# One 512-column matmul in place of two 256-column ones for the high weights of four stages

## The chip, the cores and the metric

The kernel runs on one NeuronCore of a Trainium2 chip. The metric is the device time in microseconds of one execution; smaller is better.

## What is computed

A four-layer model on one sequence of 256 tokens, 2048 channels wide, in float32. Layers 0 and 1 are gated mixers with an inner width of 4096, layers 2 and 3 are hybrid layers with three branches. The lines of the reference that touch the change:

```python
for i in range(2):                                   # layers 0 and 1
    h = rmsnorm(x, g_pre[i])
    u, z = split(h @ w_in[i])                        # each 256 x 4096
    if i == 0:
        y = pool_mixer(u, ...)    # trailing means - u, then 4 groups: d @ w_grp (1024x1024), (y + b) * scale
    else:
        y = rglru(causal_depthwise_conv(u, ...), ...)
    y = y * silu(z)
    o = y @ w_out[i]                                 # 4096 -> 2048
    x = x + rmsnorm(o, g_post[i])
    gate = sigmoid(rmsnorm(x, g_ple_in[i]) @ w_ple_gate[i])
    x = x + rmsnorm((p[i] @ w_ple[i]) * gate, g_ple_out[i])
# layers 2 and 3
    merged = sum over 3 branches of sigmoid(gate_b) * (y_b @ w_branch[b])
    x = x + merged @ w_out
```

## The kernel before

**Products.** Every matrix product has float32 accuracy from three products of numbers with fewer bits. A weight is split into a high part `w_hi` and a low part `w_lo` (what is left), an activation likewise: its tile holds the high part of 256 tokens in columns 0 to 255 and the low part in columns 256 to 511. The sum is w_hi x high + w_hi x low + w_lo x high. A tile is 128 input channels by 128 output channels. For each tile of weights the function `products` issues L589 (w_hi past the high part), L590 (w_hi past the low part) and L600 (w_lo past the high part), 256 columns each, and all three add into the same 256 columns (half) of one PSUM bank.

**Units.** The weights stream from HBM in 1144 units of 8 tiles (128 x 1024 values, 512 KB) through four slots. SyncE loads a unit into `raw`, ScalarE writes `w_hi` (`split_hi`, L1056) once PE has left the slot, and VectorE writes `w_lo` (`split_lo`, L1522) after it. Both run three units ahead of PE. Within a unit PE does all eight tiles' high matmuls first and then the eight low ones, if the tiles belong to one product.

**Stages.** A stage is a list of products, done in a number of turns. `depth` is the number of tiles that one product sums.

| stage | layers | turns x products x depth | units | who reads the product before |
|---|---|---|---|---|
| window, conv | 0, 1 | 8 x 4 x 16 | 64 | VectorE |
| pooled | 0 | 4 x 8 x 8 | 32 | VectorE, one operation: (product + b) * scale into `wide` |
| silu | 0 | 8 x 4 x 16 | 64 | VectorE times `rstd_x` into `val`, ScalarE tanh |
| lru | 1 | 4 x 24 products of two depths | 80 | both |
| squared (w_out) | 0, 1 | 4 x 4 x 32 | 64 | ScalarE: times g_post into `o_buf`, square into `val`; POOL sums |
| plain, gate | 0, 1 | | 36 | both |
| stages by token and by feature | 2, 3 | | 288 a layer | both |
| wo | 2, 3 | 4 x 4 x 16 | 32 | VectorE: `x_buf` += 0.5 * product |

In the first turn of wo, and of layer 1's squared, `first_turn` goes by input channel over the four products (L730, L732, L752 in place of L589, L590, L600); their order within a unit is the same.

**Stages by token.** gv, vb, uv, mix_gate and mix_branch have activations as the stationary operand and weights as the moving one. They use matmuls of 512 columns (L648 with `w_hi`, L665 with `w_lo`): 8 and 4 for a unit. `four_runs` reads the moving operand in runs of four columns, 32 runs for each of four weight tiles; the output is a whole bank in order. `pace` (L631) and `settle` (L610) put in one matmul of 208 or two of 128 columns whose result nobody reads.

**Order of the other engines.** In each unit ScalarE first does `split_hi` for the unit three ahead, and then what it reads for products that end in this unit (`events`). VectorE does `split_lo`, then `first` (it reads the product, L1958 in pooled, L1965 in silu, L1999 in wo), and then `second`, the rest of an earlier tile. In squared ScalarE reads twice (L1388, L1390) and POOL adds to `acc` (L2372). PE waits for a bank's last reader before it starts a product there (`occupant`). Pooled and silu rotate over four banks, squared over seven (`banks` and `pm`); wo has a list, WO_BANKS.

## Time and profile before

| | us |
|---|---|
| median of the runs | 3237.09 |
| lowest, highest of 3 | 3233.3, 3238.89 |
| span of the profiled execution | 3231.5 |
| PE (matmul) busy | 3224.2 |
| VectorE busy | 2245.0 |
| ScalarE busy | 1673.9 |
| GpSimd busy | 745.3 |

The profile is of one execution. The span runs from its first to its last instruction and holds no launch. Matmuls are pipelined: a row's duration reaches into the next matmul, so the spacing between starts tells what one costs. `x8` at the end of a row says that eight matmuls of one line were merged.

### The profile page before, as it was taken

What the parts mean: (1) busy time and instruction counts of PE and PEld (TensorE: products, weight loads), DVE (VectorE), ACT (ScalarE), POOL (GpSimd) and SP (SyncE); (2) the same over time, 40 slices, a digit from 0 to 9 for tenths busy, and PEclk for the clock granted to TensorE, in tenths of its full rate; (3) what the DMA queues carried; (4) which work ended last, traced back from release to release, by engine and by line L of the source; (5) the groups of instructions that cost most, each with busy time, mean ns of one, the idle gap of its engine ahead of it and who ended that gap; (6) DMA issues with size and microseconds to landing.
All of it is one profiled execution on the core that took longest, in us unless ns stands there. A gap on an engine that the chain in (4) does not pass through costs nothing.

```text
span 3231.5 us, 57755 instructions
## 1 busy us (share of the span) xinstructions
PE 3224.2 (100%) x24078; PEld 3067.1 (95%) x24078; DVE 2245.0 (69%) x2890; ACT 1673.9 (52%) x2082; POOL 745.3 (23%) x784
## 2 busy tenths in 40 slices
PE   9999999999999999999999999999999999999999
PEld 9999999999999999999899988889999999888889
DVE  7986654588888844887978655555568887555554
ACT  5344444565588844655655444444456554444443
POOL 2632320054544400332423200000114332000000
PEclk9999999999999999999999999999999999999999
DMA  7565665556666565555555566665665554666665
GB/s 248 183 203 191 195 225 195 178 190 216 196 194 192 196 224 194 188 191 195 169 182 170 170 196 199 193 201 193 194 201 174 177 176 157 195 196 198 194 198 174
DMA packets 171316, 621.66 MB, mean 192 GB/s; under 512 B 19376, under 2 KB 21424, under 8 KB 170672
## 3 DMA queue, kind: packets, MB, share of 16 engines
q1 hardware_dynamic: 165888, 601.96, 57.4%
q10 hardware_dynamic: 4880, 14.97, 1.2%
q8 instruction: 190, 3.11, 0.4%
q0 software_dynamic: 288, 1.05, 0.1%
q14 instruction: 70, 0.57, 0.1%
HBM read 611.61 MB, written 5.24 MB: 191 GB/s over the span
## 4 chain that ended last, share of the span: by engine, by line
PE 99%; DVE 1%; DMA 0%; ACT 0%; issue 0%; ACTq 0%; DVEq 0%
PE banks L648 20%; PE banks L600 13%; PE banks L589 13%; PE banks L590 13%; PE banks L665 10%; PE pm L600 5%; PE pm L589 5%; PE pm L590 5%; PE banks L752 2%; PE banks L730 2%; PE banks L732 2%; PE pm L752 2%; PE pm L732 2%; PE pm L730 2%; PE pm L800 0%; PE pm L926 0%
## 5 line engine op out<-in xcount | busy, mean ns | idle before, releaser
L1522 DVE TENSOR_TENSOR w_lo<-raw,w_hi 128x1024 fp32r<-128x1024 f32 x1144 | 1469.9, 1290 | 857.9 <-ACT w_hi L1056 851.5
L1056 ACT ACTIVATE w_hi<-raw 128x1024 fp32r<-128x1024 f32 x1143 | 1204.3, 1058 | 1089.7 <-PE banks L665 460.9
L589 PE MATMUL banks<-xs,w_hi 128*128 128x256 f32 x2468 | 579.4, 277 | 0.0
L590 PE MATMUL banks<-xs,w_hi 128*128 128x256 f32 x2468 | 578.1, 277 | 0.0
L648 PE MATMUL banks<-w_hi,xs 128*128 128x512 f32 x2048 | 493.5, 381 | 0.0
L590 PEld LDWEIGHTS banks<-xs,w_hi 128*128 128x128 f32 x2468 | 463.8, 188 | 0.3
L589 PEld LDWEIGHTS banks<-xs,w_hi 128*128 128x128 f32 x2468 | 463.8, 188 | 0.3
L648 PEld LDWEIGHTS banks<-w_hi,xs 128*128 128x128 f32 x2048 | 383.8, 188 | 68.2
L600 PE MATMUL banks<-xs,w_lo 128*128 128x256 f32 x2468 | 338.8, 279 | 0.0
L600 PEld LDWEIGHTS banks<-xs,w_lo 128*128 128x128 f32 x2468 | 305.7, 188 | 3.6 <-issue 2.5
L665 PE MATMUL banks<-w_lo,xs 128*128 128x512 f32 x1024 | 270.6, 384 | 0.0
L589 PE MATMUL pm<-xs,w_hi 128*128 128x256 f32 x956 | 223.3, 276 | 0.0
L590 PE MATMUL pm<-xs,w_hi 128*128 128x256 f32 x956 | 223.3, 276 | 0.0
L665 PEld LDWEIGHTS banks<-w_lo,xs 128*128 128x128 f32 x1024 | 190.2, 188 | 32.6
L590 PE MATMUL banks<-inner,w_hi 128*128 128x256 f32 x896 | 211.0, 276 | 0.0
L589 PE MATMUL banks<-inner,w_hi 128*128 128x256 f32 x896 | 211.0, 276 | 0.0
L648 PE MATMUL banks<-w_hi,y_abc 128*128 128x512 f32 x768 | 184.3, 380 | 0.0
L589 PEld LDWEIGHTS pm<-xs,w_hi 128*128 128x128 f32 x956 | 179.5, 188 | 0.0
L590 PEld LDWEIGHTS pm<-xs,w_hi 128*128 128x128 f32 x956 | 179.5, 188 | 0.0
L589 PEld LDWEIGHTS banks<-inner,w_hi 128*128 128x128 f32 x896 | 168.2, 188 | 0.0
L590 PEld LDWEIGHTS banks<-inner,w_hi 128*128 128x128 f32 x896 | 168.2, 188 | 0.0
L648 PEld LDWEIGHTS banks<-w_hi,y_abc 128*128 128x128 f32 x768 | 144.1, 188 | 24.8
(405 smaller groups left out, 5418.1 us busy)
## 6 DMA issues: line engine op xcount, KB each, us to landing
raw<-weights SPq DMA_DIRECT2D x1143, 512.0 KB, 3.6
wide<-x_in ACTq DMA_DIRECT2D x1, 2048.0 KB, 8.8
x_scratch<-wide ACTq DMA_DIRECT2D x1, 2048.0 KB, 12.5
wide<-x_scratch ACTq DMA_DIRECT2D x1, 2048.0 KB, 9.3
wide<-x_in ACTq DMA_DIRECT2D x3, 512.0 KB, 6.6
out_x<-wide SPq DMA_DIRECT2D x3, 512.0 KB, 5.4
g_v<-x_scratch ACTq DMA_DIRECT2D x2, 512.0 KB, 4.9
w_st<-w_s ACTq DMA_DIRECT2D x2, 512.0 KB, 4.6
```

Of the source, the lines that this page charges most:

```text
L589: nc.tensor.matmul(bank, w_hi[:, slot, w], x[:, 0:T], start=(k + t == 0), stop=False)
L590: nc.tensor.matmul(bank, w_hi[:, slot, w], x[:, T:2 * T], start=False, stop=False)
L600: ins = nc.tensor.matmul(bank, w_lo[:, slot, w], p.operand(i, k + t)[:, 0:T], start=False, stop=(k + t == p.depth - 1))
L648: nc.tensor.matmul(product_bank(s, i, j), x[:, at:at + P], four_runs(w_hi[:, slot, w]), start=(k == 0 and at < T), stop=False)
L665: ins = nc.tensor.matmul(product_bank(s, i, j), x[:, j * P:(j + 1) * P], four_runs(w_lo[:, slot, w]), start=False, stop=(k == depth - 1))
L730: nc.tensor.matmul(bank, w_hi[:, slot, w], operand[:, k, 0:T], start=(k == 0 and j < 4), stop=False, skip_group_check=True)
L732: nc.tensor.matmul(bank, w_hi[:, slot, w], operand[:, k, T:2 * T], start=False, stop=False, skip_group_check=True)
L752: ins = nc.tensor.matmul(bank, w_lo[:, slot, w], operand[:, k, 0:T], start=False, stop=(k == s.products[0].depth - 1), skip_group_check=True)
L1056: nc.scalar.activation(w_hi[:, slot, :], raw[:, slot, :], ACT.Copy).then_inc(hi_done, 1)
L1522: nc.vector.tensor_tensor(w_lo[:, slot, :], raw[:, slot, :], w_hi[:, slot, :].bitcast(F32), ALU.subtract).then_inc(lo_done, 1)
```

## The change

In four stages the two matmuls with the same high weights become one of 512 columns, that streams the whole activation tile (high and low part) past them. Its output is a whole bank: the high part's product in the first half, to which the low weights' product is still added, and the low part's in the second half. Whoever reads the product adds the halves. It holds for all of pooled and silu, for the first three of four turns of squared, and for all products of wo but the last; the others stay as they were. In silu, squared and wo both the moving operand and the output are addressed in runs of four columns (`in_runs`: 4 x 32 runs of 4 from each half of 256, with the same order on both sides, so that each value lands where it would without it); in pooled both are addressed in order.

The reading of a product:
- pooled: ScalarE reads the low half into `low_part` with scale and the bias `pool_shift` (= pool_b * pool_scale, made once by VectorE), VectorE waits for that (`low_read`) and does high half * scale + `low_part`.
- silu: ScalarE copies the low half, VectorE adds the high half and multiplies by `rstd_x` in a second operation, ScalarE's tanh follows in the next unit (`finish_wide`).
- squared: ScalarE copies the low half, VectorE adds into `whole`, ScalarE makes `o_buf` and the square in the next unit, POOL's sum waits for the square (`squares_made`).
- wo: VectorE updates `x_buf` twice, once with each half.

```diff
+    def wide(self, i, j):
+        if self.name == "squared":
+            return i < 3
+        if self.name == "wo":
+            return (i, j) != (3, 3)
+        return self.name in ("pooled", "silu")
...
+def in_runs(a, name):
+    return a if name == "pooled" else a.rearrange("p (g c f) -> p c g f", c=4, f=4)
...
-            stage("squared", ..., ND // 4, "p", readers="AAAA")
+            stage("squared", ..., ND // 4, "p", readers="DDDD" * 3 + "AAAA")
...
+        def whole_bank(s, i, j):
+            b = s.bank(i, j)
+            return banks[:, b, :] if b < BANKS else pm[:, b - BANKS, :]
...  (products, and likewise first_turn)
+                            if s.wide(i, j):
+                                nc.tensor.matmul(in_runs(whole_bank(s, i, j), s.name), w_hi[:, slot, w], in_runs(x, s.name),
+                                                 start=(k + t == 0), stop=False, skip_group_check=True)
+                                continue
                             nc.tensor.matmul(bank, w_hi[:, slot, w], x[:, 0:T], start=(k + t == 0), stop=False)
                             nc.tensor.matmul(bank, w_hi[:, slot, w], x[:, T:2 * T], start=False, stop=False)
...  (ScalarE)
+                        while low_parts_read:
+                            finish_wide(*low_parts_read.pop(0))
...
+                            if s.name != "wo" and s.wide(i_, j):
+                                read_low_part(i_, j)
+                                if s.name != "pooled":
+                                    low_parts_read.append((i_, j))
+                                continue
...
+                def read_low_part(i, j):
+                    m = i * s.width + j
+                    sc.wait_ge(pe_mark, product_end(s, i, j))
+                    slot = len(low_parts) % 2
+                    if len(low_parts) >= 2:
+                        sc.wait_ge(*read_of(*low_parts[-2]))
+                    low_parts.append((s, i, j))
+                    part = whole_bank(s, i, j)[:, T:2 * T]
+                    if s.name == "pooled":
+                        sc.wait_ge(shift_made, 1)
+                        ins = nc.scalar.activation(low_part[:, slot, :], part, ACT.Identity,
+                                                   scale=col("pool_scale", m), bias=pool_shift[:, m:m + 1])
+                    else:
+                        ins = nc.scalar.activation(low_part[:, slot, :], part, ACT.Copy)
+                    ins.then_inc(low_read, 1)
+
+                def finish_wide(i, j):
+                    m = i * s.width + j
+                    sc.wait_ge(*read_of(s, i, j))
+                    wait(sc, pool_done, m + (s.base["p"] - 3))
+                    if s.name == "silu":
+                        nc.scalar.activation(act[:, j % 4, :], val[:, j % 4, :], ACT.Tanh, scale=0.5)\
+                            .then_inc(act_ready, 1)
+                    else:
+                        nc.scalar.activation(o_buf[:, m, :], whole[:, j, :], ACT.Copy, scale=col(f"g_post{l}", m))
+                        nc.scalar.activation(val[:, j, :], whole[:, j, :], ACT.Square).then_inc(squares_made, 1)
...  (VectorE)
                     elif s.name == "pooled":
-                        nc.vector.tensor_scalar(wide[:, m, :], product(s, i, j), col("pool_b", m),
-                                                col("pool_scale", m), ALU.add, ALU.mult)\
+                        ve.wait_ge(low_read, low_base + m + 1)
+                        nc.vector.scalar_tensor_tensor(
+                            out=wide[:, m, :], in0=product(s, i, j), scalar=col("pool_scale", m),
+                            in1=low_part[:, (low_base + m) % 2, :], op0=ALU.mult, op1=ALU.add).then_inc(dve_read, 1)
+                    elif s.name == "silu":
+                        ve.wait_ge(low_read, low_base + m + 1)
+                        link(nc.vector.tensor_tensor(v, product(s, i, j), low_part[:, (low_base + m) % 2, :], ALU.add))
+                        nc.vector.tensor_tensor(v, v, rstd_x[:], ALU.mult).then_inc(dve_read, 1)
...
                     elif s.name == "wo":
-                        nc.vector.scalar_tensor_tensor(
-                            out=x_buf[:, m, :], in0=product(s, i, j), scalar=0.5, in1=x_buf[:, m, :],
-                            op0=ALU.mult, op1=ALU.add).then_inc(dve_read, 1)
+                        parts = [product(s, i, j)]
+                        if s.wide(i, j):
+                            parts.append(whole_bank(s, i, j)[:, T:2 * T])
+                        for part in parts:
+                            ins = nc.vector.scalar_tensor_tensor(
+                                out=x_buf[:, m, :], in0=part, scalar=0.5, in1=x_buf[:, m, :], op0=ALU.mult, op1=ALU.add)
+                            if part is not parts[-1]:
+                                link(ins)
+                        ins.then_inc(dve_read, 1)
```

## Rows read from the trace of the kernel before

**Rows 1.** The page: busy us (share of the span) xinstructions of each engine.
```profile
PE 3224.2 (100%) x24078; PEld 3067.1 (95%) x24078; DVE 2245.0 (69%) x2890; ACT 1673.9 (52%) x2082; POOL 745.3 (23%) x784
```

**Rows 2.** The page: the chain that ended last, share of the span by engine.
```profile
PE 99%; DVE 1%; DMA 0%; ACT 0%; issue 0%; ACTq 0%; DVEq 0%
```

**Rows 3.** Busy time by stretch (us, each engine (x), PEclk, DMA, GB/s): pooled, silu, squared, wo.
```profile
181.70:269.00 87.30, 87.30 (x773) 87.30 (x772) 64.06 (x93) 34.24 (x34) 6.37 (x7) 1.00 0.62 200
269.00:443.30 174.30, 174.30 (x1540) 174.30 (x1539) 115.67 (x158) 77.54 (x95) 63.28 (x61) 1.00 0.60 193
443.30:617.60 174.30, 174.30 (x1540) 174.30 (x1539) 80.79 (x69) 78.32 (x96) 14.42 (x20) 1.00 0.62 208
...
2223.20:2311.20 88.00, 88.00 (x778) 87.99 (x777) 54.57 (x65) 41.43 (x48) 2.44 (x1) 1.00 0.60 192
```

**Rows 4.** Timeline of PE in silu (start us, us, what): low matmuls of successive units.
```profile
300.96 1.07 PE L600 MATMUL banks<-xs,w_lo 128*128 128x256 f32 x8
303.68 1.07 PE L600 MATMUL banks<-xs,w_lo 128*128 128x256 f32 x8
```

**Rows 5.** Timeline of PE in mix: the pace matmul and two units after it.
```profile
1846.55 0.26 PE L631 MATMUL pm<-xs,w_hi 128*128 128x208 f32 x1
...
1847.54 1.92 PE L648 MATMUL banks<-w_hi,xs 128*128 128x512 f32 x8
...
1850.18 1.92 PE L648 MATMUL banks<-w_hi,xs 128*128 128x512 f32 x8
```

**Rows 6.** Timeline of PE where za (256 columns) gives way to mix (512).
```profile
1839.42 1.94 PE L648 MATMUL banks<-w_hi,xs 128*128 128x512 f32 x8
1841.20 1.05 PE L665 MATMUL banks<-w_lo,xs 128*128 128x512 f32 x4
1842.10 1.95 PE L648 MATMUL banks<-w_hi,xs 128*128 128x512 f32 x8
```

**Rows 7.** Timeline of PE where uv (512, settled) gives way to zc (256).
```profile
1629.50 1.05 PE L665 MATMUL banks<-w_lo,latent 128*128 128x512 f32 x4
...
1632.22 1.07 PE L600 MATMUL banks<-xs,w_lo 128*128 128x256 f32 x8
```

**Rows 8.** Timeline of PE where gv (512, unsettled) gives way to latent (256).
```profile
2405.31 1.05 PE L665 MATMUL banks<-w_lo,xs 128*128 128x512 f32 x4
...
2408.02 1.07 PE L600 MATMUL banks<-xs,w_lo 128*128 128x256 f32 x8
```

**Rows 9.** Groups by line and shape: silu, then 1742 to 1752 us in za.
```profile
L589 PE MATMUL banks<-xs,w_hi 128*128 128x256 f32 x512 | 119.2, 276 | 0.0
...
L589 PE MATMUL banks<-xs,w_hi 128*128 128x256 f32 x24 | 5.8, 281 | 0.0
```

**Rows 10.** Groups by line and shape, readers: one each of pooled, squared, wo.
```profile
L1958 DVE TENSOR_SCALAR wide<-banks,chan 128x256 f32<-128x256 f32 x31 | 16.8, 543 | 8.4 <-PE banks L600 8.3
...
L1388 ACT ACTIVATE wide<-banks,chan 128x256 f32<-128x256 f32 x9 | 4.3, 475 | 14.1 <-PE banks L600 14.1
...
L1999 DVE SCALAR_TENSOR_TENSOR wide<-banks,wide 128x256 f32<-128x256 f32 x9 | 3.7, 422 | 2.4 <-PE banks L600 2.0 <-PE pm L752 0.3
```

**Rows 11.** Groups by line and shape in silu: both splits and the reader.
```profile
L1522 DVE TENSOR_TENSOR w_lo<-raw,w_hi 128x1024 fp32r<-128x1024 f32 x64 | 78.6, 1227 | 46.9 <-ACT w_hi L1056 46.9
...
L1056 ACT ACTIVATE w_hi<-raw 128x1024 fp32r<-128x1024 f32 x64 | 67.5, 1055 | 33.0 <-PE banks L600 33.0
...
L1965 DVE TENSOR_TENSOR val<-banks,rstd_x 128x256 f32<-128x256 f32 x31 | 13.2, 426 | 10.4 <-PE banks L600 10.4
```

**Rows 12.** Timelines of ScalarE, VectorE and PE in pooled: one unit's splits and use.
```profile
195.57 1.06 ACT L1056 ACTIVATE w_hi<-raw 128x1024 fp32r<-128x1024 f32 x1 [1.66 <-PE banks L600]
...
196.66 1.23 DVE L1522 TENSOR_TENSOR w_lo<-raw,w_hi 128x1024 fp32r<-128x1024 f32 x1 [0.61 <-ACT w_hi L1056]
...
203.47 0.28 PE L589 MATMUL banks<-inner,w_hi 128*128 128x256 f32 x1
...
205.28 1.07 PE L600 MATMUL banks<-inner,w_lo 128*128 128x256 f32 x8
```

More of the change, by code:

```diff
@@ L100, in __init__, with readers_to @@
         self.by_token = name in BY_TOKEN
+    def wide(self, i, j):
[4 more added lines that the diff above has]
+        return self.name in ("pooled", "silu")
+    def readers_to(self, e, m):
+        if len(self.readers) > self.width:
+            return self.readers[:m].count(e)
+        turns, j = divmod(m, self.width)
+        return turns * self.readers.count(e) + self.readers[:j].count(e)
     def bank(self, i, j):
@@ L236, in build @@
         y_abc, merged = place("y_abc", 0, [P, 24, 2 * T], F32R), place("merged", 48, [P, ND, 2 * T], F32R)
+        low_part, whole = place("low_part", 104, [P, 2, T]), place("whole", 106, [P, 4, T])
+        pool_shift = place("pool_shift", 110, [P, NI])
         sq_sum = place("sq_sum", 40, [P, 4, T])
@@ L355, in build @@
                       readers="AAAADD" * 4)
-            stage("squared", [Product(NI, from_inner) for _ in range(4)], ND // 4, "p", readers="AAAA")
+            stage("squared", [Product(NI, from_inner) for _ in range(4)], ND // 4, "p", readers="DDDD" * 3 + "AAAA")
             stage("plain", [Product(NP_, lambda turn, k: xs[:, ND - NP_ + k, :]) for _ in range(16)], 1, "",
@@ L394, in build @@
             for e in read0:
-                read0[e] += s.turns * s.readers.count(e)
+                read0[e] += s.readers_to(e, s.turns * s.width)
             for c in s.signals.split():
@@ L454, in read_of @@
         def read_of(s, i, j):
[L456 to L457 removed]
+            m = i * s.width + j
+            e = s.readers[m if len(s.readers) > s.width else j]
+            return READ[e], s.read0[e] + s.readers_to(e, m + 1)
         def read_end(s):
@@ L600, in products @@
                             ins = nc.tensor.matmul(bank, w_lo[:, slot, w], p.operand(i, k + t)[:, 0:T],
-                                                   start=False, stop=(k + t == p.depth - 1))
+                                                   start=False, stop=(k + t == p.depth - 1),
+                                                   skip_group_check=s.wide(i, j))
                         ins.then_inc(pe_mark, 1)
@@ L729, in first_turn @@
                         bank, w = product_bank(s, j // 4, j % 4), slice(c * P, (c + 1) * P)
+                        if s.wide(0, j):
+                            nc.tensor.matmul(in_runs(whole_bank(s, 0, j), s.name), w_hi[:, slot, w], in_runs(operand[:, k, :], s.name),
+                                             start=(k == 0), stop=False, skip_group_check=True)
+                            continue
                         nc.tensor.matmul(bank, w_hi[:, slot, w], operand[:, k, 0:T], start=(k == 0 and j < 4),
@@ L1498, in _ @@
                     turn(i)
+                while low_parts_read:
+                    finish_wide(*low_parts_read.pop(0))
                 if s.name == "conv":
@@ L1957, in first @@
                     elif s.name == "pooled":
-                        nc.vector.tensor_scalar(wide[:, m, :], product(s, i, j), col("pool_b", m),
-                                                col("pool_scale", m), ALU.add, ALU.mult)\
+                        ve.wait_ge(low_read, low_base + m + 1)
[6 more added lines that the diff above has]
+                        nc.vector.tensor_tensor(v, v, rstd_x[:], ALU.mult).then_inc(dve_read, 1)
+                    elif s.name == "squared":
+                        if not s.wide(i, j):
+                            return
+                        ve.wait_ge(low_read, low_base + m + 1)
+                        if i:
+                            ve.wait_ge(squares_made, l * 12 + m - 3)
+                        nc.vector.tensor_tensor(whole[:, j, :], product(s, i, j), low_part[:, (low_base + m) % 2, :], ALU.add)\
                             .then_inc(dve_read, 1)
-                    elif s.name in ("silu", "gate", "za", "zc", "zb", "ub", "latent"):
+                    elif s.name in ("gate", "za", "zc", "zb", "ub", "latent"):
                         if s.name in ("latent", "ub"):
@@ L2235, in _ @@
                 window_rest, half_done = half_done, []
+                if s.name == "pooled":
+                    nc.vector.tensor_tensor(pool_shift, col("pool_b", 0, NI), col("pool_scale", 0, NI), ALU.mult)\
+                        .then_inc(shift_made, 1)
                 for i in range(s.turns):
                     turn(i)
+                if s.name in ("pooled", "silu", "squared"):
+                    low_base += sum(s.wide(*divmod(m, s.width)) for m in range(s.turns * s.width))
                 while half_done and s.name != "window":
@@ L2370, in post @@
                     elif s.name == "squared":
-                        gp.wait_ge(*read_of(s, i, j))
+                        if s.wide(i, j):
+                            gp.wait_ge(squares_made, l * 12 + m + 1)
+                        else:
+                            gp.wait_ge(*read_of(s, i, j))
                         nc.gpsimd.tensor_tensor(acc[:], acc[:], val[:, j, :], ALU.add).then_inc(pool_done, 1)
```

8 lines of the change are left out of this document (5 added, 3 removed).

## The prediction

> **What bounds the kernel now.** I read the page's busy line first: TensorE is busy for 3224.2 of 3231.5 us, VectorE 69%, ScalarE 52% [rows 1]. The chain that ended last agrees: 99% of it is PE [rows 2]. So the question is what one matmul costs, and whether the change makes PE wait for anybody. The table by stretch for one stage of each changed kind (the second squared and wo look the same) shows PE busy without a hole, at the full granted clock, while VectorE is idle for 23 of 87 us in pooled, 59 of 174 in silu, 94 of 174 in squared, 33 of 88 in wo, and ScalarE for more [rows 3]. So what counts is PE's spacing, from one start to the next; its "mean ns" overlaps the next matmul.
>
> Then the timeline of PE. A narrow unit (8 tiles, each two high matmuls and one low one of 256 columns) takes 303.68 - 300.96 = 2.72 us [rows 4], so 2720 / 24 = 113.3 ns per matmul. The stages by token show the 512-column form, with the moving operand already in runs of four: 12 matmuls in 1850.18 - 1847.54 = 2.64 us, 220 ns each [rows 5]. Streaming is 256/2.4 = 106.7 and 512/2.4 = 213.3 ns, so each matmul pays 6.7 ns on top, whatever its length. This is all that the change can win: 2 x 113.3 - 220 = 6.7 ns for each pair replaced.
>
> **How many.** A turn of pooled, silu, squared and wo has 8, 16, 16 and 8 units. Pooled changes in 4 turns, 32 units; silu in 4 turns of 4 products (32 tiles of 16 depth), 64; squared in 3 of 4 turns in each of two layers, 96; wo in all but the last product, 30 in each of two layers, 60. Sum 252 units of 8 pairs, 2016 pairs. At the full price: 8 x 6.7 = 53 ns a unit, 252 x 53 = 13.4 us.
>
> **What takes part of it away: the crossings.** Now all matmuls of these stages have one length. Afterwards each unit is 8 wide, then 8 narrow: it crosses from one length to the other twice. The trace has such crossings at the edges of the stages by token.
> - Narrow to wide: the first 8 wide ones after a narrow stretch take 1841.20 - 1839.42 = 1.78 us instead of 1.76, and the unit 2.68 instead of 2.64 [rows 6]: 223 ns each. The wide stream has a settled spacing (220) and an unsettled one (223), and after a narrow stretch it begins in the second. Price: 20 ns for 8.
> - Wide to narrow, from the settled spacing: from the fourth-last wide start to the 17th narrow one 1632.22 - 1629.50 = 2.72 us, where 4 x 220 + 16 x 113.3 = 2.693 [rows 7]: 27 ns.
> - Wide to narrow, from the unsettled spacing: 2408.02 - 2405.31 = 2.71 us, where 4 x 223 + 16 x 113.3 = 2.705 [rows 8]: 5 ns.
>
> In a changed unit the wide run of 8 follows a narrow run, so it is unsettled when it ends; the third row is nearer to it than the second. So a changed unit costs 8 x 220 + 8 x 113.3 + 20 + 5 = 2692 ns against 2720: **28 ns saved**, and 252 x 28 = **7.1 us**. With the second crossing at 27 ns it is 2714, 6 ns saved, 1.5 us in all. These are the ends for this term.
>
> The narrow stream has two spacings too: the groups show a mean of 276 ns where it is settled, and 281 in a stretch of za, after attention's matmuls; the difference is its spacing, some 118 against 113 [rows 9]. If the 8 low matmuls of a unit stayed there, the unit would be 8 x 223 + 8 x 118 = 2728, 8 ns more than now, 252 x 8 = +2.0 us. The rows of the crossings speak against it: there the narrow run after a wide one is back at 113 within a few matmuls.
>
> TensorE: Matmul & The Clock Gate, section Back-to-back issue gap, in the Trainium skill, gives a fixed part of about 2.5 ns for an isolated matmul, not 6.7. By that a pair saves 2.5 ns, the change 2016 x 2.5 = 5.0 us, and the time would be near 3232. The same section has a sustained spacing of some 131 ns at 512 columns; no row here is near it, the trace has 220.
>
> **What VectorE and ScalarE get to do.** All of it lies beside PE.
> - Pooled, per unit: ScalarE reads the low half with scale and bias, nearest row 0.475 us [rows 10]; VectorE's 0.543 us operation becomes one with two tensor inputs, like wo's 0.42 [rows 10]. The added wait is VectorE's, for ScalarE's read; queued behind it is the next w_lo split.
> - Silu, per two units: one copy on ScalarE (0.475 again) and one VectorE addition more (0.43, L1965's form [rows 11]); its tanh moves to the next unit.
> - Squared, per four units: a copy and an addition; o_buf and the square are made one unit later, and POOL's sum waits for them. The last turn stays narrow, so the chain after the stage starts from the same last product.
> - Wo: a second 0.42 us update per product, chained, on VectorE. The last product is narrow, so the end of the kernel is as it was.
> - pool_shift is one operation of 32 columns.
>
> Who waits for this is PE, for w_hi and w_lo. Today ScalarE's splits wait for PE, and VectorE's for ScalarE's [rows 11]. In pooled w_hi is split at 195.57 to 196.63 and w_lo at 196.66 to 197.89; PE begins the high part of that unit at 203.47 and the low part at 205.28 [rows 12]. That is 6.8 and 7.4 us ahead. ScalarE's read adds 0.5 us before a split; VectorE's wait adds that and up to one split of 1.06 us. If this cover were gone, each unit would cost what it is late. I take nothing. Per unit of pooled, the fullest case, ScalarE has 1.06 + 0.48 and VectorE 1.25 + 0.42 + a wait of about 1, of 2.69 us. No DMA is moved or added; the stages by token take a unit each 2.64 us with the same loads, so a unit each 2.69 can be fed. A bank is full 512 columns wide now, and as before it is read before its next product. So both ends of this term are 0, unless the first turn of pooled (three left-over window tiles on VectorE) catches PE once or twice: some us at most, inside the range.
>
> **Sum.** On the profiled execution: 3231.5 - 7.1 = 3224.4 us of span. Around the span lie 3237.1 - 3231.5 = 5.6 us to the median of the runs, which stay: **3230.0 us**, 0.22% less. What a measurement of this kernel can tell from no change is about 0.2%, 6.5 us, so this is just beyond it.
>
> **Rivals.**
> - *The full gain.* The wide matmuls run settled and the crossings are free: 13.4 us, 3223.7. For it: in the stages by token the settled spacing is by far the commonest, and a single matmul of another length (pace) puts a stretch there [rows 5]. The crossings seen are between moving operands of different tensors, and the output there is whole; here both differ. Against it: rows 6 and 7.
> - *Nothing is left.* Crossings at 20 + 27 and some late narrow ones: 1.5 us gained to 2.0 lost, 3235.6 to 3239.1. For it: rows 7 is a clean crossing, and its 27 ns can't be told from what a wide run of only 8 does. Against it: the wide run would have to end settled though it began unsettled.
> - *Slower: the output in runs.* In all but pooled (220 units, 1760 wide matmuls) PE now writes its product to the bank in runs of four values with a jump between. No matmul of this size in the trace writes so; only reading in such runs is shown to be free [rows 5]. If each of the 128 runs costs one more cycle, a matmul gets 128/2.4 = 53 ns longer: 1760 x 53 - 7.1 = +86 us, 3323. It turns the result to slower from about (7.1 + 6.5) us / 1760 = 8 ns per matmul, one cycle for every seventh run. PSUM — Partial Sum Buffer, section Specifications (TRN2), in the Trainium skill, speaks for it: any non-contiguous pattern is said to slow matmuls significantly, with lines of 8 bytes. A run of 16 bytes fills two such lines, so the rule may mean single values; no row here decides it.
> - *It doesn't do what it says*: a late split stalls PE. The bound above gives this no place; 0 by the rows.
>
> **Chances.** Part of the gain (the forecast) 0.47, full gain 0.25, nothing left 0.15, slower by the output 0.13. The forecast's own range is 3226 to 3236; its middle is near the 0.2% mark (3230.6), so 0.29 of its 0.47 is faster and 0.18 the same. With the full gain (0.25), faster is 0.54; with the third case, same is 0.33; slower is 0.13, since that case has it all. The range must reach to 3223.7 and to about 3239, and leaves out the slower case and a little more: 3222 to 3239.
>
> **What the profile after would show.** The spacing of L600's eight in pooled, silu, squared and wo: 2.69 us per unit if I am right, 2.667 for the full gain, 2.71 or more for nothing. Between the first wide and the first low matmul of a unit 1.78 us plus the crossing, against 1.76. Wide matmuls of pooled (output whole) and silu (in runs) side by side: if silu's are longer, the output's runs cost. PE without holes in all these stages, else my cover was wrong; and the stages by token unchanged at 2.64 and 2.68. I would be wrong if the crossings within a unit differ from those at the edges of stages.

## The result and the profile after

| | before | after |
|---|---|---|
| median of 15 runs, us | 3235.15 (3233.09 to 3238.89) | 3241.32 (3240.62 to 3243.52) |
| span of the profiled execution, us | 3231.5 | 3239.2 |

The ratio is 1.0021, 95% interval 1.0013 to 1.0028. The change made the kernel 0.2% slower; the forecast was 0.2% faster, and its range ended 2 us too low. The page after, its busy line and the chain's shares by engine; [rows 1, 2] are the same lines of before.

```profile
PE 3232.3 (100%) x22062; PEld 2993.6 (92%) x22062; DVE 2279.9 (70%) x2977; ACT 1708.7 (53%) x2170; POOL 752.8 (23%) x784
...
PE 99%; DVE 1%; ACT 0%; issue 0%; ACTq 0%; DVEq 0%
```

PE has 2016 matmuls fewer (24078 - 22062), as counted in advance, and is busy 8 us longer. The table by stretch for pooled, silu, squared and wo (from:to, us, sum and mean by engine PE, PEld, DVE, ACT, POOL, then granted clock, DMA share, GB/s); [rows 3] is before.

```profile
181.80:270.80 89.00, 89.00 (x516) 77.67 (x515) 62.50 (x94) 48.17 (x65) 6.75 (x7) 1.00 0.60 195
270.80:446.90 176.10, 176.10 (x1029) 155.49 (x1028) 129.72 (x190) 89.82 (x127) 64.49 (x62) 1.00 0.58 192
446.90:622.50 175.60, 175.60 (x1157) 160.14 (x1156) 86.15 (x82) 82.70 (x109) 17.71 (x19) 1.00 0.62 206
...
2229.40:2318.20 88.80, 88.80 (x538) 79.07 (x537) 60.79 (x80) 41.40 (x48) 2.45 (x1) 1.00 0.59 191
```

PE has no hole and the full clock in any of them, as before. Yet the stages are 1.7, 1.8, 1.3 and 0.8 us longer. So nobody makes PE wait: its own matmuls have become dearer than the halves they replace. The timeline of PE shows how: two units of pooled, then two of silu (start us, us, line, what).

```profile
231.08 1.07 PE L633 MATMUL banks<-inner,w_lo 128*128 128x256 f32 x8
232.00 2.02 PE L619 MATMUL banks<-inner,w_hi 128*128 128x512 f32 x8
233.86 1.08 PE L633 MATMUL banks<-inner,w_lo 128*128 128x256 f32 x8
...
330.57 1.09 PE L633 MATMUL banks<-xs,w_lo 128*128 128x256 f32 x8
331.49 1.99 PE L619 MATMUL banks<-xs,w_hi 128*128 128x512 f32 x8
333.32 1.09 PE L633 MATMUL banks<-xs,w_lo 128*128 128x256 f32 x8
334.24 1.99 PE L619 MATMUL banks<-xs,w_hi 128*128 128x512 f32 x8
```

From start to start a unit of pooled takes 233.86 - 231.08 = 2.78 us and one of silu 333.32 - 330.57 = 2.75, against 2.72 before [rows 4]. The eight wide ones take 233.86 - 232.00 = 1.86 us in pooled, 233 ns each, and 333.32 - 331.49 = 1.83 in silu, 229 each. Over all units of a stage the means are 2.773 (pooled) and 2.747 us (silu, the wide turns of squared, wo). So (2.773 - 2.720) x 32 + (2.747 - 2.720) x 220 = 1.7 + 5.9 = **7.6 us**, the 7.7 us of the spans. The narrow stages (2.720) and the stages by token (2.64 and 2.68) are as they were.

The spacing can be read from the groups too, by line and shape; "mean ns" is the spacing plus some 160 (380 stands for 220 in the stages by token). Pooled, silu, and mix of the kernel after:

```profile
L619 PE MATMUL banks<-inner,w_hi 128*128 128x512 f32 x186 | 47.2, 395 | 0.0
...
L619 PE MATMUL banks<-xs,w_hi 128*128 128x512 f32 x439 | 108.9, 388 | 0.0
...
L682 PE MATMUL banks<-w_hi,xs 128*128 128x512 f32 x149 | 35.8, 380 | 0.0
```

The same form, 128x512, has three mean prices: 380 where weights move past activations, 388 where activations move in runs of four, 395 where they move in order.

### The profile page after: what moved, and what is told of

Same layout as the page of the kernel before. It is cut to its first block, busy times and chain, and to the rows that moved or that the text cites. A ratio compares the mean times of both kernels' runs of the same rounds, so it can differ in the third digit from the quotient of the medians.

```text
span 3239.2 us, 54074 instructions
## 1 busy us (share of the span) xinstructions
PE 3232.3 (100%) x22062; PEld 2993.6 (92%) x22062; DVE 2279.9 (70%) x2977; ACT 1708.7 (53%) x2170; POOL 752.8 (23%) x784
## 4 chain that ended last, share of the span: by engine, by line
PE 99%; DVE 1%; ACT 0%; issue 0%; ACTq 0%; DVEq 0%
PE banks L682 20%; PE banks L633 13%; PE banks L699 10%; PE banks L619 10%; PE banks L622 8%; PE banks L623 8%; PE pm L633 5%; PE pm L623 4%; PE pm L622 4%; PE pm L619 3%; PE banks L790 2%; PE pm L790 2%; PE banks L765 1%; PE banks L768 1%; PE pm L770 1%; PE banks L770 1%
## 5 line engine op out<-in xcount | busy, mean ns | idle before, releaser
L622 PE MATMUL banks<-xs,w_hi 128*128 128x256 f32 x1956 | 460.3, 278 | 0.0
L623 PE MATMUL banks<-xs,w_hi 128*128 128x256 f32 x1956 | 459.1, 277 | 0.0
L623 PEld LDWEIGHTS banks<-xs,w_hi 128*128 128x128 f32 x1956 | 368.0, 188 | 0.3
L622 PEld LDWEIGHTS banks<-xs,w_hi 128*128 128x128 f32 x1956 | 367.8, 188 | 0.4
L619 PE MATMUL banks<-inner,w_hi 128*128 128x512 f32 x640 | 160.1, 391 | 0.0
L619 PEld LDWEIGHTS banks<-inner,w_hi 128*128 128x128 f32 x640 | 114.3, 188 | 19.7
L633 PE MATMUL pm<-xs,w_lo 128*128 128x256 f32 x956 | 129.7, 277 | 0.0
L633 PE MATMUL banks<-inner,w_lo 128*128 128x256 f32 x896 | 128.9, 278 | 0.0
```

The lines of the kernel that those rows point to most:

```text
L619: nc.tensor.matmul(in_runs(whole_bank(s, i, j), s.name), w_hi[:, slot, w], in_runs(x, s.name), start=(k + t == 0), stop=False, skip_group_ ...
L622: nc.tensor.matmul(bank, w_hi[:, slot, w], x[:, 0:T], start=(k + t == 0), stop=False)
L623: nc.tensor.matmul(bank, w_hi[:, slot, w], x[:, T:2 * T], start=False, stop=False)
L633: ins = nc.tensor.matmul(bank, w_lo[:, slot, w], p.operand(i, k + t)[:, 0:T], start=False, stop=(k + t == p.depth - 1), skip_group_check=s ...
```

## The experiments

Each edit is made to the kernel after the change, and each run was taken beside one of the kernel before on the same chip. All but e13_held are a single execution, so their units are compared, and no small difference between spans. Unit times are from start to start in PE's timeline. "In runs" is the pattern of `in_runs`, runs of four columns.

### Is it the crossing or the form?

**e1_low_wide_too**, no crossing is left:

```diff
-  matmul(bank, w_lo[:, slot, w], p.operand(i, k + t)[:, 0:T], ...)
+  matmul(in_runs(whole_bank(s, i, j), s.name), w_lo[:, slot, w],
+         in_runs(p.operand(i, k + t), s.name), ...)
```

> The low weights' matmul of the changed stages streams all 512 columns too (it adds low weights times x's low part to the second half, a small term that the reference does not need), so a changed unit is 16 wide matmuls and crosses lengths nowhere. Theory A (crossings: the wide stream is at 220 to 223 ns in long runs, and short runs of eight keep it off that): 3.52 to 3.57 us per unit in pooled, silu, squared and wo alike. Theory B (form: a wide matmul costs 228 ns in runs of four and 233 ns in order because of how it is addressed, whatever stands beside it): 3.65 us in silu, squared and wo, 3.73 us in pooled. Either way the span is longer by some 250 x 0.8 to 0.9 us = 200 to 230 us; that is not the question.

Span 3464.6 us. Timeline of PE, pooled and silu:

```profile
250.10 2.03 PE L619 MATMUL banks<-inner,w_hi 128*128 128x512 f32 x8
251.97 2.03 PE L634 MATMUL banks<-inner,w_lo 128*128 128x512 f32 x8
...
400.50 1.97 PE L619 MATMUL banks<-xs,w_hi 128*128 128x512 f32 x8
402.30 1.98 PE L634 MATMUL banks<-xs,w_lo 128*128 128x512 f32 x8
```

(251.97 - 250.10) / 8 is 233 ns, (402.30 - 400.50) / 8 is 225. Over many units the means are firmer: a unit is 3.733 us in pooled and 3.627 in silu, squared and wo: 16 x 233.3 and 16 x 226.7. With only one length of matmul the high price stays. Theory A (crossings), which had 3.52 to 3.57, falls. The 226.7 is a mean: from start to start the single matmuls of e1's silu take 220, 224, 227, 233 and 229 ns, over and over, and those of its pooled 231 and 236 in turn.

**e2_two_halves** keeps the changed readers and the bank halves, but fills them with two 256-column matmuls:

```diff
-  matmul(in_runs(whole_bank(s, i, j), s.name), w_hi[:, slot, w], in_runs(x, s.name), ...)
+  for half in (slice(0, T), slice(T, 2 * T)):
+      matmul(whole_bank(s, i, j)[:, half], w_hi[:, slot, w], x[:, half], ...)
```

> Everything as in the changed kernel, its readers and waits too, but the wide matmul is split into two of 256 columns, one into each half of the bank. Theories A and B (the time comes from PE's spacing): 2.72 us per unit in the four stages and a span of 3231 to 3233 us, as before the change. Theory C (the readers' extra work on ScalarE and VectorE disturbs PE): units stay at 2.745 us or more and the span at 3239 us.

Its table by stretch for pooled and silu:

```profile
181.70:269.00 87.30, 87.30 (x773) 87.30 (x772) 62.41 (x94) 48.67 (x65) 6.93 (x8) 1.00 0.61 197
269.00:443.30 174.30, 174.30 (x1540) 174.30 (x1539) 129.86 (x190) 89.91 (x127) 63.32 (x62) 1.00 0.60 195
```

PE is busy for the whole of both windows, and as many matmuls fell into them as before (773 and 1540 [rows 3]), with ScalarE at 48.67 and 89.91 us instead of 34.24 and 77.54: a unit is 2.720 us again. So all that the change gave VectorE and ScalarE costs nothing here. The span is 3235.1 because of one stage: wo of layer 3 runs at 2.827 us a unit. Its group, where one line issues both halves, and then that of the kernel before:

```profile
L620 PE MATMUL banks<-merged,w_hi 128*128 128x256 f32 x224 | 28.7, 281 | 0.0
```
```profile
L589 PE MATMUL banks<-merged,w_hi 128*128 128x256 f32 x120 | 27.9, 276 | 0.0
```

That is the unsettled narrow spacing, 118 ns, seen in za of before [rows 9]: 32 units x 0.107 = 3.4 us. In wo of layer 2 the same matmuls take 2.720 us a unit. Why this one stage fell into it, one execution can't tell.

### Which side of the pattern?

**e3_patterns** turns the patterns about. Pooled now reads and writes in runs, silu only reads so, squared neither, wo only writes so (silu and wo then put values at the wrong tokens, which changes no time):

```diff
-  return a if name == "pooled" else a.rearrange("p (g c f) -> p c g f", c=4, f=4)
+  return a.rearrange("p (g c f) -> p c g f", c=4, f=4) if name in ("pooled", "silu") else a
+def out_in_runs(a, name):
+  return a.rearrange("p (g c f) -> p c g f", c=4, f=4) if name in ("pooled", "wo") else a
```

> Each stage gets another way of addressing its wide matmul: pooled reads and writes in runs of four, silu reads in runs and writes in order (its values land at other tokens, so what follows is computed on permuted values), squared reads and writes in order, wo reads in order and writes in runs (permuted too). Theory A: all units 2.75 us, the addressing does not matter. Theory B: pooled falls from 2.773 to 2.747 us, squared rises from 2.746 to 2.773 us, and silu and wo tell which side it hangs on: silu near 2.747 and wo near 2.773 if it is the read, the other way round if it is the write. If writing in runs costs by itself, silu is the fastest of all, near 2.69 us.

Groups in pooled, silu, squared, wo:

```profile
L624 PE MATMUL banks<-inner,w_hi 128*128 128x512 f32 x188 | 46.9, 388 | 0.0
...
L624 PE MATMUL banks<-xs,w_hi 128*128 128x512 f32 x438 | 108.7, 388 | 0.0
...
L624 PE MATMUL banks<-inner,w_hi 128*128 128x512 f32 x216 | 54.6, 395 | 0.0
...
L624 PE MATMUL banks<-merged,w_hi 128*128 128x512 f32 x96 | 24.3, 395 | 0.0
```

388 wherever it reads in runs, 395 wherever it reads in order; units 2.747 and 2.773 us. How it writes makes no difference. The rival that priced the output in runs is refuted: its price is 0. PSUM — Partial Sum Buffer, section Specifications (TRN2), in the Trainium skill, has any non-contiguous pattern slow a matmul significantly; for runs of four fp32 values the trace disagrees, 388 against 388.

**e4_two_units** streams two units' high weights (16 wide), then two units' low ones (16 narrow), in the stages whose products are deep enough: half the crossings.

```diff
+  while s.wide(i, j) and p.depth >= 2 * UNIT_TILES and k < p.depth:
+      for half in range(2): ...   # 8 wide matmuls each, then
+      for half in range(2): ...   # 8 narrow ones each
```

> In silu, squared and wo (not in the first turn by rows) PE does the wide matmuls of two units and then the low ones of both, so lengths are crossed half as often. A unit of 8 x 220 + 8 x 113.3 would take 2.667 us, and takes 2.747. Theory A: half of the 80 ns goes, 2.707 us per unit, the span about 6 us shorter than that of the changed kernel. Theory B (228 ns per wide matmul by its form, crossings cost only the 16 ns seen in the low ones): 2.739 us per unit, the span about 1 us shorter.

Timeline of PE in silu:

```profile
331.55 3.79 PE L617 MATMUL banks<-xs,w_hi 128*128 128x512 f32 x16
335.18 1.99 PE L629 MATMUL banks<-xs,w_lo 128*128 128x256 f32 x16
337.00 3.79 PE L617 MATMUL banks<-xs,w_hi 128*128 128x512 f32 x16
```

Wide: (335.18 - 331.55) / 16 = 227 ns, still not 220. Two units take 337.00 - 331.55 = 5.45 us, 2.726 each against 2.747: each pair of crossings taken out gave 42 ns, and 5452 - 16 x (226.7 + 113.3) = 12 ns is left for the pair that stays. The unit lies between what theory A had (2.707) and theory B (2.739). So crossings cost tens of ns a unit, as assumed, and with half of them gone the unit is still dearer than the 2.720 of before: what ate the gain is the wide matmul. Span 3236.7.

### Why 220 by token, and 227 or 233 here?

In the stages by token weights move past loaded activations; here it is the other way about. Theory D: it is the place in SBUF of what moves against what is loaded. In before and after `xs`, `inner` and `merged` start 64 B below the weights, modulo 512 B (`w_hi` starts at 128, `xs` and `inner` at 64). So in the stages by token, with the roles exchanged, the moving operand is at +64. Four kernels only put spare columns ahead of buffers, and a fifth, e12, does so and changes reads as well. `inner_offset` also moves what shares the space of `inner`, as `y_abc` and `latent`. The edits, in fp32 columns:

```diff
# e5_shift_plus64: all three at +64 B
-  sb("xs_offset", [P, 112])
+  sb("xs_offset", [P, 144])
# e6_shift_0_m128: xs 0, inner and merged -128 B
+  sb("xs_offset", [P, 128])   # and sb("inner_offset", [P, 96])
# e7_shift_m32_p32: xs -32, inner and merged +32 B
+  sb("xs_offset", [P, 120])   # and val_offset 8, sb("inner_offset", [P, 24])
# e9_inner_p32: xs as it was, inner and merged +32 B
+  sb("inner_offset", [P, 24])
# e12_p96_all_runs: inner and merged +96 B, all reads of wide units in runs
+  sb("inner_offset", [P, 40])
```

> The runs so far: a wide matmul costs 226.7 ns in runs of four and 233.3 in order, whatever it writes and whatever stands beside it, but the stages by token (weights moving, activations loaded) have 220 in runs. In SBUF the activations xs and inner start 64 bytes below the weights, counted modulo 512 bytes; so for a wide matmul the moving operand lies at -64 from the loaded one, in the stages by token at +64. Here xs, inner and merged are moved to +64. Theory D (the spacing hangs on this distance): silu, squared and wo come to 220 ns per wide matmul, 2.68 us a unit; the stages by token, now at -64, go to 226.7, 2.72 us a unit. Theory E (it hangs on what kind of tensor moves, or on nothing of place): no stage moves by more than 0.01 us a unit.

> xs at 0 from the weights modulo 512 bytes, inner and merged at -128. Theory D: silu (xs), squared, wo and pooled (inner, merged) change, and the narrow stages too; two distances show whether it is the sign or the size. Theory E: nothing moves: pooled 2.773, silu, squared and wo 2.747, narrow 2.72, by token 2.64 us a unit.

> xs at -32 bytes from the weights, inner and merged at +32. Theory D: the narrow stages on xs (window, gate, conv) leave 2.72 us a unit, and silu and squared leave 2.747 in different directions. Theory E: nothing moves.

> The changed kernel with xs where it is (-64 bytes from the weights modulo 512) and only inner, merged and their neighbours at +32. Theory D: silu (xs) stays at 2.747 us a unit; squared's changed turns and wo come to 2.707, as when both were moved, and the narrow units that read inner (the last turn of squared) go to about 2.80; pooled, read in order, 2.80. Window, conv and gate stay at 2.72 us. The sum over the changed units is some 2 us shorter than in the changed kernel, and the narrow ones lose 2 x 16 x 0.08 = 2.6 us and some in lru. Theory E: nothing moves.

> As e10_p32_all_runs with inner and merged at +96 in place of +32. If only the distance modulo 64 bytes counted, it equals e10_p32_all_runs; -64, 0 and +64 gave different spacings, so I expect it differs, by 0.02 to 0.1 us a unit in pooled, squared and wo. Silu, on xs, is as in e10_p32_all_runs.

What they measured, us per unit:

| kernel | span | narrow, on xs | silu | squared, wide | pooled |
|---|---|---|---|---|---|
| after (-64) | 3239.2 | 2.720 | 2.747 | 2.747 | 2.773 |
| e5 (+64) | 3309.2 | 2.827, later 2.720 | 2.767 | 2.767 | 2.73 to 2.78 |
| e6 (xs 0, inner -128) | 3340.6 | 2.880 | 2.760 | 2.760, 2.738 | 2.81 |
| e7 (xs -32, inner +32) | 3298.3 | 2.840 | 2.760 | 2.707 | 2.800 |
| e9 (inner +32) | 3256.4 | 2.720 | 2.747 | 2.707 | 2.800 |
| e12 (inner +96) | 3259.3 | 2.720 | 2.707 | 2.747 | 2.747 |

No instruction is added or taken in any of the first five rows, and yet every spacing moves. Narrow matmuls on `xs` at -64 (rows 9), at +64 and at 0, the last two here (window of e5, window of e6):

```profile
L622 PE MATMUL banks<-xs,w_hi 128*128 128x256 f32 x132 | 31.8, 279 | 0.0
```
```profile
L624 PE MATMUL banks<-xs,w_hi 128*128 128x256 f32 x127 | 31.2, 283 | 0.0
```

276, 279 and 283: 113.3, 118 and 120 ns. The 120 of xs at 0, and the 118.3 at -32 (e7), hold in window, gate and conv alike, whatever settle does there: they hang on the place. The 118 at +64 does not hang on it alone, for in conv of e5 it ends at the settle pair (L644). PE's timeline around it:

```profile
784.81 0.28 PE L623 MATMUL banks<-xs,w_hi 128*128 128x256 f32 x1
...
786.34 0.33 PE L644 MATMUL ms_bank<-xs,w_hi 128*128 128x128 f32 x2
...
787.48 0.28 PE L622 MATMUL banks<-xs,w_hi 128*128 128x256 f32 x1
...
789.29 1.07 PE L633 MATMUL banks<-xs,w_lo 128*128 128x256 f32 x8
```

Thirteen matmuls before the pair take 786.34 - 784.81 = 1.53 us, 118 ns each; sixteen after it take 789.29 - 787.48 = 1.81 us, 113 each. The unit is 2.827 us up to there and 2.720 from there on, as in gate. So at +64 the narrow form has the same two spacings as at -64, where za of before had the 118; in the window stage of e5 it stays at 118 in spite of the settle pair there.

The stages by token moved too. The weights moving in mix of e5, now at -64, early in the stage and later:

```profile
1883.43 1.07 PE L699 MATMUL banks<-w_lo,xs 128*128 128x512 f32 x4
...
1886.15 1.07 PE L699 MATMUL banks<-w_lo,xs 128*128 128x512 f32 x4
...
2010.09 1.09 PE L699 MATMUL banks<-w_lo,xs 128*128 128x512 f32 x4
...
2012.87 1.09 PE L699 MATMUL banks<-w_lo,xs 128*128 128x512 f32 x4
```

At first a unit takes 2.72 us, 12 x 226.7, as expected, and its single matmuls follow each other after 220, 224, 227, 233 and 229 ns: the cycle of e1's silu, with the roles exchanged and the same distance. After some 35 units it goes to 2.78 us, and each mix takes 16.8 us more. The wide form in squared of e7, at +32:

```profile
L620 PE MATMUL banks<-inner,w_hi 128*128 128x512 f32 x227 | 55.0, 382 | 0.0
```

So the place counts, for both forms and in both roles. But silu at +64 did not come down to 220 as expected (e5: 2.767, with its low matmuls at 118). e12 was to tell whether the distance counts modulo 64 B, where +32 and +96 would be one. They aren't: squared takes 2.747 us a unit in e12, and 2.720 in the same kernel at +32 (e10, below).

**e15_all_wide_p64** joins e1's edit with e5's shift, so that no narrow matmul disturbs the wide ones:

> As e1_low_wide_too (the low matmuls 512 columns wide too, no crossing) with xs, inner and merged at +64 bytes from the weights and not -64. If the place is all that makes the stages by token fast: silu, squared and wo at 16 x 220 = 3.52 us a unit (3.63 at -64), and the stages by token, now at -64, at 12 x 226.7 = 2.72. If role or tensor matters besides, silu stays above 3.57 us.

Timeline in silu:

```profile
400.66 1.92 PE L619 MATMUL banks<-xs,w_hi 128*128 128x512 f32 x8
402.42 1.92 PE L634 MATMUL banks<-xs,w_lo 128*128 128x512 f32 x8
404.18 1.92 PE L619 MATMUL banks<-xs,w_hi 128*128 128x512 f32 x8
```

(404.18 - 400.66) / 16 = **220.0 ns**, against 226.7 in e1, which differs from it by the place alone. With activations moving, 220 is to be had at +64 with reading in runs. Squared of layer 0 takes 3.520 us a unit too; that of layer 1 takes 3.56 before its settle and 3.520 after it, and wo, which has no settle, 3.573 (223 ns each): the place allows the 220, and the state decides whether it is had. The stages by token came to the 2.720 expected only in part, as in e5 (the span is 3505.0, 40 us above e1's). Pooled, in order, stays at 233.3 in both, but for 3.66 us a unit before its settle in e15.

Is it the distance, or where one of the two lies? Modulo 512 B, silu of e1 (moving operand at 64 B, loaded one at 128) and mix of e5 (moving 128, loaded 192) share the cycle of 226.7; mix of before (moving 128, loaded 64) and silu of e15 (moving 192, loaded 128) share the 220. Neither the moving nor the loaded one's own place sorts these four, the distance does.

**e14_load_64** asks whether the load of the next weights is what the reading collides with. Each wide matmul after a product's first loads and computes only 64 of the 128 output channels, so that the other 64 lack most of the high part:

```diff
-  matmul(in_runs(whole_bank(s, i, j), s.name), w_hi[:, slot, w], in_runs(x, s.name), ...)
+  n_out = HALF if k + t else P
+  matmul(in_runs(whole_bank(s, i, j)[0:n_out], s.name), w_hi[:, slot, w][:, 0:n_out], in_runs(x, s.name), ...)
```

> The changed kernel, but outside first_turn the wide matmuls (all but the first tile of a product) load and compute only the first 64 of 128 output channels, so the other 64 lack most of the high part; the low ones are whole. The moving operand and its 512 columns are as they were. If the extra time of a wide matmul is its read meeting the next weight load, seven in eight wide ones come down: from 233 towards 220 to 227 ns in pooled (2.67 to 2.72 us a unit) and from 228 towards 220 to 224 in silu. If it is the moving read by itself, both stay: 2.773 and 2.747 us a unit.

Pooled and silu:

```profile
L620 PE MATMUL banks<-inner,w_hi 128*64 128x512 f32 x165 | 42.2, 394 | 0.0
...
L620 PE MATMUL banks<-xs,w_hi 128*64 128x512 f32 x413 | 101.3, 384 | 0.0
```

In silu half a load takes 388 to 384, some 224 ns of spacing, which is what a collision was to give; in pooled it takes next to nothing (395 to 394, 232 ns), which is not. That neither shows nor excludes the collision.

### What a unit's pattern hangs on

**e8_low_in_runs** and **e11_all_runs** read the low matmuls of wide units in runs too, e11 pooled as well:

```diff
-  matmul(bank, w_lo[:, slot, w], p.operand(i, k + t)[:, 0:T], ...)
+  matmul(runs(bank), w_lo[:, slot, w], runs(p.operand(i, k + t)[:, 0:T]), ...)
```

> The changed kernel, with the low weights' matmuls of the changed products (outside first_turn) addressed in runs of four as well. If reading in runs costs by itself, as it does against the 220 of the stages by token, the eight low ones take 8 x 120 and not 8 x 115, and a unit of silu 2.79 us. If the 16 ns that the low ones lose after the wide ones come from the change of addressing, they go, and it is 2.73 us. Theory B holds either way for pooled: its wide ones stay at 233 ns.

> No tensor moved; in the four stages both the wide and the low matmuls read in runs of four, pooled and first_turn too. Pooled falls from 2.773 to 2.707 us a unit, as silu did, wo and squared stand between 2.707 and 2.747 (two repeating patterns). Span 3232 to 3235 us, about that of the kernel before.

Spans 3236.4 and 3240.5 (e11 was expected at 3232 to 3235). Both expectations for silu in e8 were too high (2.79 or 2.73): it comes to 2.707. Now a stage has two patterns, and `settle`'s two 128-column matmuls change one for the other. In e8 the settle of silu helps: a unit takes 275.56 - 272.81 = 2.75 us before it and 283.99 - 281.28 = 2.71 after. In e11 pooled goes from 2.720 to 2.707 at its settle, but silu comes in at 2.707 and goes at its settle, after the third unit, from 2.707 to 2.753 and 2.794 in turn, and stays there to the end of the stage. Timeline of e11 around that settle (L645):

```profile
272.29 1.96 PE L619 MATMUL banks<-xs,w_hi 128*128 128x512 f32 x8
274.09 1.06 PE L634 MATMUL banks<-xs,w_lo 128*128 128x256 f32 x8
274.99 1.96 PE L619 MATMUL banks<-xs,w_hi 128*128 128x512 f32 x8
276.80 0.33 PE L645 MATMUL ms_bank<-xs,w_hi 128*128 128x128 f32 x2
276.97 1.14 PE L634 MATMUL banks<-xs,w_lo 128*128 128x256 f32 x8
277.94 2.01 PE L619 MATMUL banks<-xs,w_hi 128*128 128x512 f32 x8
279.79 1.07 PE L634 MATMUL banks<-xs,w_lo 128*128 128x256 f32 x8
```

The eight wide ones take 276.80 - 274.99 = 1.81 us before it and 279.79 - 277.94 = 1.85 after it. So the same pair at the same spot does good or harm by the pattern that it meets. The narrow last turn of squared in layer 1 was left unsettled likewise (2.827 instead of 2.720, 16 units, 1.7 us).

**e10_p32_all_runs** is e11 with e9's shift:

> As e9_inner_p32, and in the four stages both the wide and the low matmuls read in runs of four, pooled too. Theory D with the low ones in runs as they helped silu (2.747 to 2.707 us): silu 2.707, squared, wo and pooled at 8 x 221 + 8 x 113 to 116 = 2.67 to 2.70 us. Span 3230 to 3234 us.

Pooled, squared and wo came to 2.720, silu to 2.707, but each mix takes 6.9 us more: span 3250.8. Of the two tensors loaded there one, `y_abc`, moved, and its units went from 2.640 us to between 2.71 and 2.73; those on `xs`, which did not move, went to 2.67 and 2.68 as well. So a place that is good for one role can be bad for the other, and a stretch at a bad place unsettles its neighbours.

**e13_held** is e11 with the settles put where they help:

```diff
-  (0, "silu", 0, 2): "enter", (0, "squared", 1, 4): "enter",
+  (0, "squared", 3, 0): "enter", (1, "squared", 3, 0): "enter", (2, "wo", 3, 6): "enter",
```

> All wide and low matmuls of the four stages in runs of four as in e11_all_runs, where pooled went to 2.707 us a unit after its settle matmuls and silu from 2.707 to 2.75/2.79 after its own. Here the settle pairs of silu and of layer 0's squared are taken out, and one is put in where the narrow last turn of squared starts and in the last product of layer 2's wo. If settle sets the pattern: silu and squared's changed turns stay at 2.707, the narrow last turns at 2.72 and not 2.827; the span is 3228 to 3231 us and the ratio to the kernel before 0.999 to 1.000. If the pattern is set by something else, silu is again at 2.75 to 2.79 us a unit and the span at 3236 us or more.

Timeline in silu:

```profile
330.17 1.06 PE L635 MATMUL banks<-xs,w_lo 128*128 128x256 f32 x8
331.07 1.96 PE L620 MATMUL banks<-xs,w_hi 128*128 128x512 f32 x8
332.87 1.06 PE L635 MATMUL banks<-xs,w_lo 128*128 128x256 f32 x8
```

Silu, the wide turns of squared in layer 0, wo, and pooled and layer 1's squared after their settles all take 2.707 us a unit; before those settles it is 2.720, as in the narrow last turns. The eight wide ones take 332.87 - 331.07 = 1.80 us, less than 8 x 226.7: the single starts give 223, 224, 222, 224, 227, 233, 229 and 220 ns, of which the last five are e1's cycle and the first three, behind the narrow ones, are cheaper. Span 3229.8; **3231.77 us** (3231.34 to 3233.59, 11 runs) against 3236.86 (3233.11 to 3238.68, 15 runs) for the kernel before, ratio 0.9987, 95% interval 0.9978 to 0.9996. It beats both kernels, the one before by 0.1%. Of the 13 ns a unit, some 220 units get their share: 2.9 us, of which the new settles and crossings take some; the spans of the two profiled executions differ by 3231.5 - 3229.8 = 1.7. The rest of the 5.1 us between the medians lies in how executions scatter, and no trace here shows what scatters: the runs of e13 lie within 2.3 us, those of before within 5.6.

## Why the prediction was wrong

- *PE bounds, and nothing else gets near it*: right. No holes, full clock, and in e2, with every added reader, copy and wait, the units are 2.720 us as before.
- *How many*: right, 252 units; 7.6 us over them explain the 7.7 of the spans.
- *The price of the 512-column form*: **this step failed.** The prediction took 220 ns from rows 5, where the weights move, for matmuls where the activations move. Measured: 226.7 in runs and 233.3 in order (e1). For a unit of silu that is 8 x 6.7 = 53 ns, exactly the whole gain; for one of pooled 8 x 13.3 = 107, twice the gain. The text saw that "here both differ", operands and output, and yet priced neither end of it. It looked for a price only in the output in runs, which costs nothing (e3), and let rows 5 stand for the input. A row of a form is only a price for that form in that role, place and reading order.
- *The crossings*: for silu the size was right, 25 ns predicted and 2747 - 8 x (226.7 + 113.3) = 27 left over, but not its parts: 20 + 5 were to fall on the wide and the low ones, and the single starts give 10 + 16. In pooled 0 was left over. These are remainders; e4, with half of them gone, bears silu's out (42 + 12 = 54 for two units). With the gain eaten up, they took silu below zero. The sum again: silu 2692 + 53 + 2 = 2747, pooled 2692 + 107 - 25 = 2774; over 220 and 32 units that is 12.1 + 2.6 = 14.7 us, the distance of the forecast span (3224.4) from the measured one (3239.2).
- *5.6 us around the span*: wrong too. After has 3241.12 - 3239.2 = 1.9 us around it, and before has the same: its executions beside e13 have spans of 3235.1 and 3232.2 at times of 3236.86 and 3233.99. So the other 3.7 us lay inside the span: executions of before differ by that much, and the profiled one was short. What differs in them no trace of before shows; e2's wo, 3.4 us longer with the same matmuls, is of that size. That was luck for the forecast: the span was missed by 14.8 us, the time (3230.0 against 3241.32) by 11.3.
- *Rivals*: full gain, refuted. Output in runs, refuted. "Nothing is left" came nearest (3239.1 at its upper end), but by luck, since its sum had other terms. The slower side had one mechanism only, the wrong one; a wide spacing of its own for moving activations was missing from the list, and so from the range.
- The rows to look at named in advance did show it at once: L600's eight at 2.71 or more, silu against pooled (the other way round from the rival with the output in runs: pooled, whose output is whole, was dearer).

Where the pattern comes from stays partly open. Shown: reading order (e3), place (e1 against e15; e6 and e7 for the narrow form), and the state that settle leaves (e5's conv, e8, e11, e13) each change the spacing. Not shown: that the load of the next weights is the other party (e14 is mixed), why reading in order stays at 233.3 at +64 as well, and what puts a stage into one state or the other, as silu of e5 (2.767) beside that of e15. The shifts also move buffers that other engines use; that e9, which moved inner's neighbours, left silu at 2.747 speaks against these, and no run excludes them.

## What to carry to other kernels

Before two matmuls are joined to one longer one, read the spacing of the long form with the same tensor moving and the same one loaded; if the trace has none, its price is unknown by as much as the gain of joining or more (6.7 ns a pair here, against 6.7 to 13.3 of difference). Where PE has no holes, move one buffer by 32 to 128 B and measure again, every stage that uses it: that adds no instruction and cost a stage up to 6% (2.720 to 2.880 us a unit) or won it 3% (3.627 to 3.520 in silu of e15). Here every kernel with a moved buffer took longer as a whole (3250.8 us of span or more), since other stages lost more than that. Spacing that was stabilised by hand, with settles, has to be stabilised anew when the stream around it changes.

## What the hardware showed

- At the full clock the mean spacing of matmuls of one shape took a few values: 220, 226.7 and 233.3 ns for 512 columns, 113.3, 118 and 120 for 256. The cheapest two differ by 220 - 113.3 = 106.7 ns for 256 columns, which leaves 6.7 on top in each; the dearest have 13.3 (256) and 20 (512). With the moving operand in runs of four and long stretches of one length, the distance in SBUF of the moving from the loaded operand told 226.7 (-64 B: silu of e1, mix of e5 at first) from 220 (+64 B: silu of e15, mix of before), whichever of the two was the weights. In order it was 233.3 at both, once settled.
- The 226.7 is a cycle of five spacings, 220 to 233 ns, and not the price of a single matmul (e1, e5); among narrow ones eight of them can come out cheaper than 8 x 226.7 (1.80 us in e13).
- TensorE: Matmul & The Clock Gate, section Step-by-step: what each phase is for, in the Trainium skill, says that loading the next weights takes no read bandwidth from the running matmul. If only the length counted, e1 and e15 would be the same; the wide matmuls of silu differ by 6.7 ns each. Whether the load is the cause, e14 left open.
- Writing to PSUM in runs of 16 B is as fast as in order (e3).
- Two matmuls of 128 columns change the spacing of a stage to its end, from 2.707 to 2.77 us a unit on average (silu of e11); the same two helped pooled there, by 13 ns a unit, and silu of e8, from 2.75 to 2.707.
